# Banded attention of a two-layer encoder: the query squares in two parts, a later sum, and an earlier output

## The reference, cut to what matters

```python
def rms_norm(x, g):
    y = x * rsqrt(mean(x * x, axis=-1) + EPS)
    return y * g

q = rms_norm(q.reshape(B, S, 16, 64), q_norm)     # mean of 64 squares for each head and position
# chunk c of 64 positions reads chunks c-1 and c of the shared k and v
s = q @ k.T * 64 ** -0.5 - slopes * dist
mx = max(max(s), sink)
p = exp(s - mx)
p = p / (sum(p) + exp(sink - mx))
o = p @ v
```

## Time and profile before

| | |
|---|---|
| median of three runs | 1452.02 us |
| the profiled execution | 1451.81 us, of which the span of instructions is 1450.0 us |
| PE busy | 1419.7 us, 98% of the span |
| DVE busy | 556.5 us, 38% |
| ACT busy | 577.1 us, 40% |
| POOL busy | 550.8 us, 38% |
| chain that ended last | PE 93%, DVE 3%, ACT 2% |

### The profile page before, as it was taken

One profiled execution on the slowest core, in us unless ns is written; L12 is line 12 of the kernel. 1 busy time (PEld: TensorE's weight loads), 2 busy tenths in 40 slices (PEclk: granted clock), 3 DMA queues, 4 the chain that ended last, 5 costly groups with the idle time before them and its releaser, 6 DMA issues.

```text
span 1450.0 us, 24344 instructions
## 1 busy us (share of the span) xinstructions
PE 1419.7 (98%) x9400; PEld 1147.2 (79%) x9400; DVE 556.5 (38%) x1058; ACT 577.1 (40%) x987; POOL 550.8 (38%) x268
## 2 busy tenths in 40 slices
PE   5999999999999999999999999999999999999998
PEld 5977777777777888888888887778788888888887
DVE  3555666666644222220122225774322221022210
ACT  5654445545535242232223334875334232223221
POOL 2542333232322444344434444122345344434432
PEclk9999999999999999999999999999999999999999
DMA  6331111111110423233232243111233323422232
GB/s 234 122 112 60 60 60 45 59 44 46 52 56 25 124 95 105 89 90 109 97 106 78 80 125 95 45 49 45 77 109 102 102 69 102 135 87 88 76 93 78
DMA packets 39230, 124.15 MB, mean 86 GB/s; under 512 B 4192, under 2 KB 5472, under 8 KB 39136
## 3 DMA queue, kind: packets, MB, share of 16 engines
q1 hardware_dynamic: 38976, 122.55, 26.6%
q10 hardware_dynamic: 160, 0.26, 0.1%
HBM read 120.44 MB, written 2.10 MB: 85 GB/s over the span
## 4 chain that ended last, share of the span: by engine, by line
PE 93%; DVE 3%; ACT 2%; issue 1%; DMA 0%; DVEq 0%; SPq 0%; ACTq 0%
PE bank L623 79%; PE bank L953 1%; ACT ws L1256 1%; PE bank L824 1%; PE bank L981 1%; DVE ws L1723 1%; DVE ws L1720 1%; DVE act_lo L1720 1%; PE bank L801 1%; PE bank L1188 1%; PE bank L635 1%; PE bank L1212 1%; PE bank L870 1%; PE bank L1199 1%; PE bank L970 0%
## 5 line engine op out<-in xcount | busy, mean ns | idle before, releaser
L563 POOL TENSOR_TENSOR w_lo<-w_raw,w_hi 128x1024 fp32r<-128x1024 f32 (+1 forms) x248 | 529.8, 2152 | 770.5 <-ACT w_hi L1256 770.5
L623 PE MATMUL bank<-act_hi,w_hi 128*128 128x512 f32 (+1 forms) x1776 | 709.1, 399 | 3.9 <-DVE act_lo L1720 2.6
L623 PE MATMUL bank<-act_hi,w_lo 128*128 128x512 f32 (+1 forms) x1776 | 680.5, 383 | 0.0
L623 PE MATMUL bank<-act_lo,w_hi 128*128 128x512 f32 (+1 forms) x1776 | 679.8, 383 | 0.0
L623 PEld LDWEIGHTS bank<-act_hi,w_hi 128*128 128x128 f32 x1776 | 335.4, 189 | 71.3 <-issue 4.6
L623 PEld LDWEIGHTS bank<-act_hi,w_lo 128*128 128x128 f32 x1776 | 335.0, 189 | 65.6
L623 PEld LDWEIGHTS bank<-act_lo,w_hi 128*128 128x128 f32 x1776 | 335.8, 189 | 58.5 <-issue 2.9
L1256 ACT ACTIVATE w_hi<-w_raw 128x1024 fp32r<-128x1024 f32 (+1 forms) x248 | 228.7, 952 | 92.7 <-PE bank L623 90.6
L1714 DVE TENSOR_TENSOR ws<-bank,ws 128x512 f32<-128x512 f32 x110 | 75.9, 691 | 333.9 <-PE bank L623 323.7
L1256 ACT ACTIVATE ws<-ws 128x512 f32<-128x512 f32 (+2 forms) x120 | 79.7, 665 | 157.9 <-DVE ws L1714 111.8
L2062 DVE TENSOR_TENSOR xT<-xT,bank 128x512 f32<-128x512 f32 (+1 forms) x48 | 33.0, 687 | 258.2 <-PE bank L623 258.2
(11 more groups left out here) (178 smaller groups left out, 957.9 us busy)
## 6 DMA issues: line engine op xcount, KB each, us to landing
w_raw<-w_stream SPq DMA_DIRECT2D x154, 512.0 KB, 3.3
w_raw<-w_out SPq DMA_DIRECT2D x32, 384.0 KB, 3.2
w_raw<-w_down SPq DMA_DIRECT2D x32, 384.0 KB, 3.1
w_raw<-w_down SPq DMA_DIRECT2D x32, 320.0 KB, 3.1
ws<-x_in SPq DMA_DIRECT2D x1, 2048.0 KB, 8.5
ws<-mem_in SPq DMA_DIRECT2D x2, 512.0 KB, 4.8
out<-ws SPq DMA_DIRECT2D x1, 1024.0 KB, 4.2
out<-ws SPq DMA_DIRECT2D x1, 768.0 KB, 3.6
```

The source lines that it names most:

```text
L563: nc.gpsimd.tensor_tensor(w_lo[:, s, 0:width * P], w_raw[:, s, 0:width * P], w_hi[:, s, 0:width * P].bitcast(F32), ALU.subtract).then_inc( ...
L623: mm = nc.tensor.matmul(acc, wt[:, c % RING, wsl], at[:, act0(k0 + k), off:off + n], start=(start and k == 0 and m == 0), stop=(stop and k ...
```

## The change

The sum of the query squares is no longer one float32 matmul over a float32 tile. ScalarE writes the squares rounded into act_hi, slot 16. GpSimd squares w(0) itself into w(1) and subtracts the rounded squares to make the lower part, in act_lo, slot 16 (`sw_split`). TensorE then sums with two fp32r matmuls, against a square of ones that ScalarE copies into act_lo, slot 17, once. In TensorE's order the sums of unit u + 1 come after step k = 2 of the product in place of k = 0, and the output of unit u - 1 directly after k = 0. The remaining edits rename or merge semaphores.

```diff
+        SQ_HL = 16
+        ones64_r = act_lo[:, 17, 0:P]
...
+            def sw_split(u):
+
+                pool.wait_ge(S.acc_free, TILE0["swq"] + u + 1)
+                nc.gpsimd.tensor_tensor(w(1), w(0), w(0), ALU.mult).then_inc(S.sw_prod, 1)
+                pool.wait_ge(S.sw_prod, u + 1)
+                pool.wait_ge(S.sw_sq, u + 2)
+                if due(u):
+                    pool.wait_ge(S.sw_ss, u)
+                nc.gpsimd.tensor_tensor(act_lo[:, SQ_HL, :], w(1), act_hi[:, SQ_HL, :].bitcast(F32),
+                                        ALU.subtract).then_inc(S.squares_lo, 1)
+
             for name, count in _order[5:]:
-                lower_all(name, count)
+                if name == "swq":
+                    swq = BLOCK0[name]
+                    for j in range(3):
+                        lower(0, swq + j, KT)
+                    sw_split(0)
+                    lower(0, swq + 3, KT)
+                    sw_split(1)
+                    for u in range(SW_U):
+                        if u + 2 < SW_U:
+                            sw_split(u + 2)
+                        lower(0, swq + u + 4, KT)
+                elif name != "mq1":
+                    lower_all(name, count)
...
             def sw_sums(u):
-                pe.wait_ge(S.sw_sq, u + 1)
+                pe.wait_ge(S.squares_lo, DN_HEADS - 1 + u + 1)
                 if due(u):
                     pe.wait_ge(S.sw_q, u)
-                nc.tensor.matmul(psum(D[4]), sq(ONES64), w(1), start=True, stop=True).then_inc(S.sw_ss, 1)
+                nc.tensor.matmul(psum(D[4]), ones64_r, act_hi[:, SQ_HL, :], start=True, stop=False)
+                nc.tensor.matmul(psum(D[4]), ones64_r, act_lo[:, SQ_HL, :], start=False, stop=True
+                                 ).then_inc(S.sw_ss, 1)
...
             pe.wait_ge(S.b_lo, KT)
+            pe.wait_ge(S.pick_done, 3)
             sw_project(0, range(KT))
...
             for u in range(SW_U):
                 sw_project(u + 2, range(0, 1))
+                if u > 0:
+                    sw_output(u - 1)
+                sw_project(u + 2, range(1, 3))
                 if u + 1 < SW_U:
                     sw_sums(u + 1)
-                if u > 0:
-                    sw_output(u - 1)
-                sw_project(u + 2, range(1, 4))
+                sw_project(u + 2, range(3, 4))
                 sw_transposes(QPB * u)
...
             act.wait_ge(S.block_used, BLOCK0["kv"])
+            a(ones64_r, sq(ONES64), ACT.Copy).then_inc(S.pick_done, 1)
...
-                a(w(1), w(0), ACT.Square).then_inc(S.sw_sq, 1)
+                a(act_hi[:, SQ_HL, :], w(0), ACT.Square).then_inc(S.sw_sq, 1)
```

More of the change, by code:

```diff
@@ L245, in yoco_kernel @@
             o_sum = sem("o_sum")
-            osq_lo = sem("osq_lo")
+            squares_lo = sem("squares_lo")
             oss = sem("oss")
@@ L279, in yoco_kernel @@
             f_lo = sem("f_lo")
-            kv_sq = sem("kv_sq")
             kv_ss = sem("kv_ss")
@@ L290, in yoco_kernel @@
             sw_sq = sem("sw_sq")
+            sw_prod = sem("sw_prod")
             sw_ss = sem("sw_ss")
@@ L742, in output_sums @@
             def output_sums(h):
-                pe.wait_ge(S.osq_lo, h + 1)
+                pe.wait_ge(S.squares_lo, h + 1)
                 two_part_sums(D[0], act_lo[:, OHI_T, :], act_lo[:, OLO_T, :]).then_inc(S.oss, 1)
@@ L1155, in _ @@
             product(0, BLOCK0["kv"] + 1, KT, 0, lambda k: k, psum(1), True, True)
-            pe.wait_ge(S.kv_sq, 1)
+            pe.wait_ge(S.sw_sq, 1)
             pe.wait_ge(S.r_ln, 2)
@@ L1636, in _ @@
             act.wait_ge(S.acc_free, TILE0["kv"] + 1)
-            a(w(3), w(2), ACT.Square).then_inc(S.kv_sq, 1)
+            a(w(3), w(2), ACT.Square).then_inc(S.sw_sq, 1)
             act.wait_ge(S.kv_ss, 1)
@@ L1877, in split_o @@
                     dve.wait_ge(S.oss, h)
-                sub(act_lo[:, OLO_T, :], psum(D[0]), act_lo[:, OHI_T, :].bitcast(F32)).then_inc(S.osq_lo, 1)
+                sub(act_lo[:, OLO_T, :], psum(D[0]), act_lo[:, OHI_T, :].bitcast(F32)).then_inc(S.squares_lo, 1)
             def o_finish(h):
```

## The result

The changed kernel takes 1459.67 us (median of five runs, 1458.05 to 1461.27) against 1452.02 us of the kernel before in five runs beside them. The ratio is 1.0061, its 95% interval [1.0051, 1.0072]: slower, by 7.7 us in the medians and by 7.4 to 10.5 us by the interval. The forecast was 1461.5 us.

A forecast was written before the change was run, and what follows sets the result against it. The softmax chain (5.97 us) nearly equals TensorE's work (6.06), so lengthening it costs time. First sums 2.2, first turn 0.6 and six turns 6.7 make 9.5; 1451.8 + 9.5 + 0.2 = 1461.5 us, range 1454 to 1464.

The forecast's parts named there:

- What bounds the loop: Full turns: softmax chain 5.97 us against TensorE's 6.06, so a shorter TensorE gains at most 0.09 us a turn.
- The hold of VectorE: Loop turns: VectorE's small operations, including the joining with the sink, stand until GpSimd's instruction ends; a turn grows 1.11 us.
- rival A: Loop: the joining is free, only the sum of the denominator is held; turn 10.60 us, 1459.0 us in all; chance 0.27.
- rival B: Loop: GpSimd holds nothing of VectorE; 1453.7 us, no change that can be told; chance 0.11.
- One sign that the prediction named: VectorE in the profile after: L2183's form far over 0.16 us on average, in six of sixteen cases, ending with a GpSimd instruction.
- the first turn: Loop's first turn: a split without a lowering behind it, first joining ends 0.62 late; costs 0.6 us.
- The size of a turn: Full turns: next scores at T + 10.91, grown by 1.11 us; six turns cost 6.7 us.
- the product of the split: GpSimd's split: an f32 tensor_tensor of 128x512 takes 1.28 us, running from T + 0.87 to T + 2.15.
- The first sums: Before the loop: sums wait for GpSimd's lowering and split, 2.70 us later, less 0.49 for shorter sums: +2.2 us.
- the lower bound of 1.3: First sums: cost only 1.3 us if the split's product starts with the raw tile, before the lowering's end.
- rival D: First sums: the long wait lowers TensorE's clock, next product at 1.2 GHz takes 5.5 us more; 1467 us; chance 0.05.
- The copy of the ones: ScalarE, ahead of the eight upper parts: 0.305 us, costs nothing; 0.3 if the cover by GpSimd's lowering fails.

The follow-up runs named there:

- the kernel with upper parts only: Changed kernel without GpSimd's split, sums one fp32r matmul over the rounded squares, lower part left out: 1449.75 us, ratio 0.9994.
- idle instructions: Kernel before plus two GpSimd instructions per unit in the split's places, their results used by nobody: 1456.59 us, ratio 1.0036.
- the kernel with the swapped queue: Changed kernel with the lowering ahead of the split in GpSimd's queue: 1455.61 us, ratio 1.0039.
- later first sums: Changed kernel with the first sums issued behind steps k = 0 to 3 of unit 1's product: 1455.06 us, ratio 1.0031.
- all three together: Changed kernel with lowering held back, first sums behind four steps of unit 1's product, one more product step before each turn's first transposes: 1447.91 us, ratio 0.9985.
- the one with the late lowering: Changed kernel with each lowering behind a split held back until VectorE's second division of the turn: 1456.91 us, ratio 1.0049.
- the last experiment: Kernel before, two more product steps before first transposes in first and last turn, first sums behind two steps of unit 1's product: 1448.84 us, ratio 0.9986.

## Why the prediction was right, and where its sizes were off

**What bounds the loop: right.** That a shorter TensorE gains at most 0.09 us a turn is shown by the kernel with upper parts only: 0.72 us less work in a turn, 0.02 us less time.

**The hold of VectorE: right, shown.** The choice between the forecast and rival A was whether the joining is held. It is, in the changed kernel (0.62 and 0.96 us), with idle instructions (0.38 and 1.07) and by each of GpSimd's three instructions; moved away, 0.23. Rival A and rival B are out. By the Trainium skill ("SBUF — State Buffer", "Who interferes with whom") tensor_scalar can enter the mode that takes the lock. The trace agrees in that the joining was held, even with four elements a partition; in which mode it ran no row shows.

One sign that the prediction named can't come if its forecast holds: the denominator's form (L2183, now L2214) with a mean far over 0.16 us in six of sixteen cases. In the forecast's own order the denominator comes behind the second joining, when the lowering is over, and so it was: 0.15 to 0.17 us in all cases. That sign fits rival A. The joining was long in thirteen cases, but not all near 0.9: six of 0.62, six of 0.96, and 0.70 in the first turn.

**The size of a turn: 10.91 forecast, 10.70 measured.** The term mis-sized is the product of the split, taken as 1.28 us from the earlier trace rows. It took 1.04. The form was that of the earlier trace rows, but those eight multiply two different tiles and this one a tile by itself. The split and the lowering behind it end 0.24 earlier, and with them the second joining: at T + 5.66, where the sum had 5.94 plus up to 0.05. From there the steps held: 5.04 us to the next scores, 4.97 forecast. Six turns gave 5.4 us for 6.7, the first turn 0.5 for 0.6.

**The first sums: the queue holds GpSimd, as forecast; 2.0 us for 2.2.** The clean reading is that of the kernel with the swapped queue, at full clock. The first sums start there 4.04 us after the eight transposes ahead of them, 1.61 before: 2.43 later, where the forecast had 2.70. The difference is again the product's 0.24. Up to the first scores 2.0 us are left of it.

The profiled execution of the changed kernel itself reads otherwise, and would mislead:

```profile
893.72 2.39 POOL L566 TENSOR_TENSOR w_lo<-w_raw,w_hi 128x1024 fp32r<-128x1024 f32 x1 [11.58 <-ACT w_hi L1286]
896.99 1.04 POOL L615 TENSOR_TENSOR ws<-ws 128x512 f32<-128x512 f32 x1 [0.88 <-DVE ws L1745]
```

The lowering ended at 896.11, and the product waited for the raw tile until 896.99. But this raw tile is itself 1.6 us late by the half clock ahead of it. In the three profiles of the changed queue without the half clock (later first sums, swapped queue, all three together) the product stands directly behind the lowering. So the queue does exclude the lower bound of 1.3.

**The clock: rival D came in part.** It was priced as a whole product at 1.2 GHz, 5.5 us, with a chance of 0.05. In the profiled execution two stretches cost 1.6 us each on TensorE and 2.5 together in the span, one of them behind a wait that before has too. That it belongs to the change isn't shown. Of ten profiles two (the changed kernel, and the one with the late lowering) show it in the banded part, at both waits; with the longest wait, 3.0 us, it didn't come. The profile of the kernel before has such a stretch elsewhere, which the prediction didn't look at: the granted clock was 0.50 from 52 to 54 us, with a wait of 2.1 us ahead of 50.74. And the medians don't carry it: the mean granted clock of the profiled execution is 0.995, that of the changed kernel's other four 0.998 or 0.999, as before. By the Trainium skill ("TensorE: Matmul & The Clock Gate", Part 1) idling sends the array back to 1.2 GHz; here it did so in some executions and not in others of like waits.

**The copy of the ones: nothing, as forecast.** The eight lower parts it could have pushed back took 8.03 us, from 878.63, where the earlier trace rows show 8.22.

The forecast was too high in the six turns by 1.3, in the first turn by 0.1 and at the first sums by 0.2. Off the 9.5 this leaves 7.9, and the medians show 7.7. That the profiled execution's 1461.27 us is so near the forecast's 1461.5 is luck: what the sum had too much, the clock made up. One term, the product of the split, stands behind nearly all of it.

## What to carry to other kernels

Before work goes to an idle GpSimd, look at what VectorE does at that moment. Here a tensor_scalar within SBUF, and an operation with two inputs in SBUF, stood still until GpSimd's instruction ended, even with four elements a partition. A tensor_reduce from SBUF (0.69 us) and operations with an input in PSUM (0.69 and 0.74 us) kept their times. A long GpSimd instruction belongs beside those, or where VectorE waits. And shortening an engine gives nothing where another chain ends within a tenth of a microsecond of it: fill its waits with work first, as the last experiment does.

## What the runs showed of the hardware beyond the forecast

- GpSimd multiplies a 128x512 f32 tile by itself in 1.04 us, and takes 1.27 to 1.28 with two different tiles (and the subtraction here). All of the changed kernel's, by form (count, busy us, mean ns, idle before):

```profile
L620 POOL TENSOR_TENSOR act_lo<-ws,act_hi 128x512 fp32r<-128x512 f32 x8 | 10.2, 1274 | 0.6
L615 POOL TENSOR_TENSOR ws<-ws 128x512 f32<-128x512 f32 x8 | 8.3, 1040 | 41.0 <-DVE ws L1745 41.0
```

- A VectorE operation that is held gets in between two GpSimd instructions that stand back to back (927.69 to 927.77 in the kernel with the swapped queue), and doesn't hold the second back: 0.08 us lie between the two, as in the changed kernel, where nothing got in.
- At a granted clock of 0.50 a matmul of 128x512 (fp32r) has a pitch of 0.43 us, for 0.228 at 1.00.
